# Second block's latent, pool and convolution projections from three products of split operands, quarter by quarter

## The reference, cut to what matters

```python
h = rmsnorm_2(x, norm1_g[l]) * (1.0 + sc1) + sh1          # (256, 1024)
proj = h @ w_in[l]                                         # (1024, 5792)
cq, ckv, kr, pu, cx, cb, cc, gl = jnp.split(proj, IN_OFFSETS, axis=-1)
ya = mla_branch(cq, ckv, kr, ...)      # latent attention, 384 + 256 + 32 columns
yb = pool_branch(pu, ...)              # 512 columns
yc = conv_branch(cx, cb, cc, ...)      # 3 x 512 columns
gates = sigmoid(gl + b_gate)           # 3 x 1024 columns
```

## Time and profile before

| | us |
|---|---|
| median of 3 runs | 2551.68 |
| lowest, highest | 2546.58, 2554.73 |
| the profiled execution's own time | 2548.41 |
| span of its instructions | 2546.4 |
| TensorE matmuls busy | 2051.8 |
| VectorE busy | 864.3 |
| ScalarE busy | 594.8 |

### The profile page before, as it was taken

One profiled execution on the slowest core, in us unless ns is written; L12 is line 12 of the kernel. 1 busy time (PEld: TensorE's weight loads), 2 busy tenths in 40 slices (PEclk: granted clock), 3 DMA queues, 4 the chain that ended last, 5 costly groups with the idle time before them and its releaser, 6 DMA issues.

```text
span 2546.4 us, 34316 instructions
## 1 busy us (share of the span) xinstructions
PE 2051.8 (81%) x14184; PEld 1362.8 (54%) x14184; DVE 864.3 (34%) x1599; ACT 594.8 (23%) x1001; POOL 32.0 (1%) x50
## 2 busy tenths in 40 slices
PE   7877889998998997999876666665999976666765
PEld 6756657877756885788542222222778652222221
DVE  4645564665554664244220000002144230010002
ACT  3222234441123442064210010001054120000000
POOL 0010000000000000000000000000000000000000
PEclk9989899998998998999888887887999988888787
DMA  8201034766963665432459999999332439999996
GB/s 309 102 1 35 2 109 155 265 242 208 329 240 137 251 250 176 149 133 100 165 223 427 426 427 425 426 427 387 134 132 93 201 153 426 427 426 427 426 426 283
DMA packets 150299, 641.76 MB, mean 252 GB/s; under 512 B 9310, under 2 KB 30840, under 8 KB 117046
## 3 DMA queue, kind: packets, MB, share of 16 engines
q1 hardware_dynamic: 143898, 637.13, 63.0%
q10 hardware_dynamic: 6300, 3.20, 0.5%
HBM read 639.21 MB, written 1.10 MB: 251 GB/s over the span
## 4 chain that ended last, share of the span: by engine, by line
PE 55%; DMA 31%; DVE 6%; ACT 3%; issue 2%; DVEq 1%; POOL 1%; SPq 0%; ACTq 0%; POOLq 0%
DMA ring<-in_w_down 31%; PE psum L1189 5%; PE psum L844 5%; PE psum L846 5%; PE psum L845 5%; PE psum L1304 4%; PE psum L1100 3%; PE psum L1089 3%; PE psum L942 3%; PE psum L616 2%; PE psum L1179 2%; PE psum L823 2%; PE psum L647 1%; PE psum L959 1%; PE psum L737 1%
## 5 line engine op out<-in xcount | busy, mean ns | idle before, releaser
L1284 PE MATMUL psum<-ring,arena 128*32 128x256 f32 x4096 | 298.0, 442 | 185.1 <-DMA ring<-in_w_up 146.1
L1284 PEld LDWEIGHTS psum<-ring,arena 128*32 128x32 f32 x4096 | 143.5, 123 | 341.5 <-issue 155.6
L1304 PE MATMUL psum<-ring,arena 128*32 128x512 f32 x1024 | 166.9, 784 | 94.1 <-DMA ring<-in_w_down 84.8
L844 PE MATMUL psum<-arena_r 128*128 128x512 f32 x512 | 207.8, 406 | 13.9 <-DVE arena_r L1650 7.1
L846 PE MATMUL psum<-ring_r,arena_r 128*128 128x512 f32 x512 | 205.0, 400 | 0.0
L1991 DVE TENSOR_TENSOR arena<-psum,arena 128x256 f32<-128x256 f32 x32 | 13.6, 425 | 559.0 <-PE psum L1284 559.0
L1384 DVE TENSOR_TENSOR ring_r<-ring,arena_r 128x2048 fp32r<-128x2048 f32 x64 | 143.8, 2288 | 87.0 <-ACT arena_r L2049 87.0
L2392 ACT ACT_TABLE_LOAD x32 | 41.1, 1283 | 514.3 <-PE psum L1284 514.3
L1998 DVE COPY arena<-psum 128x512 f32<-128x512 f32 x64 | 44.3, 692 | 273.0 <-PE psum L1304 271.8
L2049 ACT CAST arena_r<-ring 128x2048 fp32r<-128x2048 f32 x64 | 119.6, 1904 | 71.8 <-PE psum L846 71.8
L1304 PEld LDWEIGHTS psum<-ring,arena 128*32 128x32 f32 x1024 | 32.8, 126 | 191.4 <-DMA ring<-in_w_down 101.5
(11 more groups left out here) (379 smaller groups left out, 3026.1 us busy)
## 6 DMA issues: line engine op xcount, KB each, us to landing
ring<-in_w_gate SPq DMA_DIRECT2D x64, 2048.0 KB, 26.6
ring<-in_w_up SPq DMA_DIRECT2D x64, 2048.0 KB, 26.1
ring<-in_w_down SPq DMA_DIRECT2D x64, 2048.0 KB, 26.3
ring<-in_mlp_w SPq DMA_DIRECT2D x32, 2048.0 KB, 8.7
ring<-in_w_mod SPq DMA_DIRECT2D x24, 2048.0 KB, 11.2
ring<-in_w_in SPq DMA_DIRECT2D x20, 2048.0 KB, 8.1
ring<-in_gdn_w_in SPq DMA_DIRECT2D x8, 2048.0 KB, 17.9
ring<-in_dswa_w_in SPq DMA_DIRECT2D x9, 1536.0 KB, 14.4
```

Of the source, the lines that this page charges most:

```text
L844: mm(o, xh, wh, start=start, stop=False, skip_group_check=True)
L1284: ins = mm(PS[32 * j:32 * j + 32, 4 + m, 0:T], XGE[:, 4 * u + kk, :], W(v + 2 * m + u, D)[:, kk, j * T:(j + 1) * T], start=u == 0 and kk = ...
L1304: ins = mm(PS[32 * j:32 * j + 32, (7, 4)[half], :], HTE[:, k % 2, 32 * (k // 2):32 * (k // 2) + 32], W(v + 4 + u, D)[:, j, half * 512:(hal ...
```

## The change

All projections of that group but the first (`V_CQ`, which stays float32) are computed as three fp32r products, as the gates are. The weights are split quarter by quarter: 5 ring units with 4 quarters each make 20 quarters per layer, numbered q = 0 to 19. For the two units that `tok` computed (`V_KV`, `V_PU`) a quarter is two of the eight 128-row chunks over all columns; for the other three a quarter is 128 columns over all rows. ScalarE casts a quarter into one of three buffers (`WP`, in parts of the arena that hold other things later), VectorE writes the rest in place into the slot, TensorE waits for the count of `w_lo` and multiplies. A buffer is reused when TensorE has signalled the quarter three before (`half_used`, or the slot's release at a unit's last quarter). VectorE also makes the low part of the activations, `HL_R`, in an area of its own ahead of everything else; the later subtraction into `HT_R` (L1866) stays. The counts of `hi` and `w_lo` that the gates wait for are raised by 20 per layer. Nothing is changed in SyncE's and GpSimd's streams.

```diff
+        hl_at = q_at + 4 * T + 4 * 258
+        P1_UNITS = ((V_KV, C_PU - QR), (V_PU, 512), (V_CX, 512), (V_CC, 512), (V_CB, 512))
+        NQ = 4 * len(P1_UNITS)
+        WP = [gr_at, mixt_at, ot_at]
+        HL_R = ar_r[:, hl_at:hl_at + KC * T].rearrange("p (k n) -> p k n", k=KC)
...
+        def part_high(q):
+            w, wide = WP[q % 3], P1_UNITS[q // 4][1]
+            if q < 8:
+                return ar_r[:, w:w + 2 * wide].rearrange("p (k c) -> p k c", k=2)
+            return ar_r[:, w:w + KC * P].rearrange("p (k c) -> p k c", k=KC)
+        def part_of(slot, q):
+            wide, j = P1_UNITS[q // 4][1], q % 4
+            v = slot[:, 0:KC * wide].rearrange("p (k c) -> p k c", k=KC)
+            return v[:, 2 * j:2 * j + 2, :] if q < 8 else v[:, :, j * P:(j + 1) * P]
...
         @block.tensor
...
+                def three(o, a, b, start, stop):
+                    (ah, al), (bh, bl) = a, b
+                    mm(o, ah, bh, start=start, stop=False, skip_group_check=True)
+                    mm(o, al, bh, start=False, stop=False, skip_group_check=True)
+                    return mm(o, ah, bl, start=False, stop=stop, skip_group_check=True)
+                def part_done(ins, q):
+                    if q % 4 == 3:
+                        used(ins, u2 + P1_UNITS[q // 4][0])
+                    else:
+                        ins.then_inc(sem("half_used"), 1)
+                def tok_split(i, b):
+                    w = P1_UNITS[i][1]
+                    for q in range(4 * i, 4 * i + 4):
+                        pe.wait_ge(sem("w_lo"), L * (NQ + 24) + q + 1 + 64)
+                        wh, wl = part_high(q), part_low(q)
+                        for t in range(TT):
+                            ts = slice(t * P, (t + 1) * P)
+                            for kk in range(2):
+                                k = 2 * (q % 4) + kk
+                                ins = three(bank(b + t, w), (XH_R[:, k, ts], HL_R[:, k, ts]), (wh[:, kk, :], wl[:, kk, :]),
+                                            k == 0, k == KC - 1)
+                            if q % 4 == 3 and t == 0:
+                                ins.then_inc(sem("tok_mm"), 1)
+                        part_done(ins, q)
-                def feat(n, b):
-                    full(pe, u2 + n, tu)
-                    for ch in range(4):
+                def feat(i, b):
+                    for q in range(4 * i, 4 * i + 4):
+                        pe.wait_ge(sem("w_lo"), L * (NQ + 24) + q + 1 + 64)
+                        wh, wl = part_high(q), part_low(q)
+                        o = pair(b + (q % 4) // 2, T)[:, q % 2]
                         for k in range(KC):
-                            ins = mm(pair(b + ch // 2, T)[:, ch % 2], W(u2 + n, 512)[:, k, ch * P:(ch + 1) * P], HT[:, k, :],
-                                     start=k == 0, stop=k == KC - 1, skip_group_check=True)
-                    used(ins, u2 + n)
+                            ins = three(o, (wh[:, k, :], wl[:, k, :]), (XH_R[:, k, :], HL_R[:, k, :]), k == 0, k == KC - 1)
+                        part_done(ins, q)
                 tok(V_CQ, QR, 0)
-                tok(V_KV, C_PU - QR, 2)
-                tok(V_PU, 512, 4)
-                feat(V_CX, 6)
+                tok_split(0, 2)
+                tok_split(1, 4)
+                feat(2, 6)
                 pe.wait_ge(sem("ckv_out"), L + 1)
                 pe.wait_ge(sem("sq2"), L + 1)
-                feat(V_CC, 0)
-                feat(V_CB, 2)
+                feat(3, 0)
+                feat(4, 2)
...
         @block.vector
...
+                dve.wait_ge(sem("x_hi"), L + 1)
+                v.tensor_tensor(HL_R, HT[:], XH_R.bitcast(F32), ALU.subtract)
+                def part_rest(q):
+                    dve.wait_ge(sem("hi"), L * (NQ + 24) + q + 1 + 64)
+                    v.tensor_tensor(part_low(q), part_weight(q), part_high(q).bitcast(F32), ALU.subtract).then_inc(sem("w_lo"), 1)
+                for q in range(3):
+                    part_rest(q)
                 for t in range(TT):
...
                     v.tensor_copy(CQ[:, t, 0:QR], bank(t, QR)).then_inc(sem("cq_out"), 1)
+                for q in range(3, 6):
+                    part_rest(q)
...
                 ins.then_inc(sem("ckv_out"), 1)
+                part_rest(6)
+                part_rest(7)
                 dve.wait_ge(sem("sq2"), L + 1)
...
+                part_rest(8)
                 dve.wait_ge(sem("rs2"), L + 1)
...
                 ins.then_inc(sem("cqn_ready"), 1)
+                part_rest(9)
+                part_rest(10)
...
                     v.tensor_copy(MK[:, t, :, NOPE:DQK], bm(KR[:, t, :], MH))
+                for q in range(11, 18):
+                    part_rest(q)
                 dve.wait_ge(sem("cx_out"), L + 1)
                 spent(dve, u2 + V_CC, tu)
...
                 settle()
+                part_rest(18)
                 for ch in range(4):
                     v.tensor_scalar(BCT[:, ch, :], CZ[:, ch, 0:T], CW[:, ch:ch + 1], None, ALU.mult)
+                part_rest(19)
...
                 ins.then_inc(sem("conv_y"), 1)
-                dve.wait_ge(sem("x_hi"), L + 1)
                 v.tensor_tensor(HT_R[:], HT[:], XH_R.bitcast(F32), ALU.subtract).then_inc(sem("x_lo"), 1)
...
         @block.scalar
...
+                def part_high_of(q):
+                    if q % 4 == 0:
+                        full(act, u2 + P1_UNITS[q // 4][0], tu)
+                    if q >= 3:
+                        p = q - 3
+                        if p % 4 == 3:
+                            spent(act, u2 + P1_UNITS[p // 4][0], tu)
+                        else:
+                            act.wait_ge(sem("half_used"), L * 3 * len(P1_UNITS) + 3 * (p // 4) + p % 4 + 1 + 32)
+                    a.copy(part_high(q), part_weight(q)).then_inc(sem("hi"), 1)
+                for q in range(3):
+                    part_high_of(q)
                 for i, (b, w) in enumerate(((0, QR), (2, KVR))):
+                    if i == 1:
+                        for q in range(3, 7):
+                            part_high_of(q)
...
                 a.copy(ajunk[:], SS2[:, 3:4]).then_inc(sem("sq2"), 1)
+                for q in range(7, 11):
+                    part_high_of(q)
...
                 ins.then_inc(sem("pu_out"), 1)
+                for q in range(11, 15):
+                    part_high_of(q)
...
                 ins.then_inc(sem("cx_out"), 1)
+                for q in range(15, NQ):
+                    part_high_of(q)
```

More of the change, by code:

```diff
@@ L321, in program @@
         PU = c(TT, 512)
+        mixt_at = c.at
         MIXT = c(4, T)
         BCT = c(4, T)
+        ot_at = c.at
         OT = c(4, T)
@@ L328, in program @@
         KT = c(MH, T)
+        hl_at = q_at + 4 * T + 4 * 258
+        assert hl_at + KC * T <= 20480
+        P1_UNITS = ((V_KV, C_PU - QR), (V_PU, 512), (V_CX, 512), (V_CC, 512), (V_CB, 512))
+        NQ = 4 * len(P1_UNITS)
+        WP = [gr_at, mixt_at, ot_at]
+        HL_R = ar_r[:, hl_at:hl_at + KC * T].rearrange("p (k n) -> p k n", k=KC)
         c = Carve(sec_top)
@@ L535, in W, with part_weight, part_low @@
             return ring[n % RING][0:parts, 0:a * b].rearrange("p (a b) -> p a b", b=b)
+        def part_high(q):
[7 more added lines that the diff above has]
+            return v[:, 2 * j:2 * j + 2, :] if q < 8 else v[:, :, j * P:(j + 1) * P]
+        def part_weight(q):
+            return part_of(ring[(U_SEC + P1_UNITS[q // 4][0]) % RING], q)
+        def part_low(q):
+            return part_of(ring_r[(U_SEC + P1_UNITS[q // 4][0]) % RING], q)
         def gate_weight(s):
@@ L1182, in gate @@
                             used(ins, wu)
-                    pe.wait_ge(sem("w_lo"), L * 24 + s + 1 + 64)
+                    pe.wait_ge(sem("w_lo"), L * (NQ + 24) + NQ + s + 1 + 64)
                     if s == 0:
@@ L1864, in _ @@
                 ins.then_inc(sem("conv_y"), 1)
-                dve.wait_ge(sem("x_hi"), L + 1)
                 v.tensor_tensor(HT_R[:], HT[:], XH_R.bitcast(F32), ALU.subtract).then_inc(sem("x_lo"), 1)
                 def gate_rest(s):
-                    dve.wait_ge(sem("hi"), L * 24 + s + 1 + 64)
+                    dve.wait_ge(sem("hi"), L * (NQ + 24) + NQ + s + 1 + 64)
                     v.tensor_tensor(gate_low(s), gate_weight(s), WQ[s % 3].bitcast(F32), ALU.subtract).then_inc(sem("w_lo"), 1)
```

## The result

| | median us | runs (lowest to highest) |
|---|---|---|
| before | 2551.98 | 4 (2546.58 to 2554.73) |
| changed | 2519.39 | 4 (2518.50 to 2525.24) |

The ratio is 0.9878, 95% interval 0.9862 to 0.9894: 32.6 us faster between the medians, with 27 to 35 us in the interval. The forecast was 2528 with a range of 2521 to 2540. The profiled execution took 2518.50 us (span 2516.5), 29.9 less than the one before.

A forecast was written before the change was run, and what follows sets the result against it. TensorE alone was taken to bound the projections: 62.94 us removed, 51.6 added, 11.35 gained per layer, 22.7 for two. That gave 2525.7 from the profile, 2529.0 from the median; forecast 2528, range 2521 to 2540.

The forecast's parts named there:

- TensorE alone bounds the stretch, and the stretch gains the difference of its instructions: Projections: TensorE sets the end, the other engines have room; gain 11.35 us per layer, 22.7 us for two.
- The sum of the changed part: TensorE work added per layer in the projections: 34.08, 11.15 and 6.36 us, sum 51.6 us, replacing 62.94 us.
- The 288 columns: Key/value products: 48 of 288 columns at 132.6 ns, on a line between two measured widths, 6.36 us per layer.
- the subtractions of 576 elements: VectorE's rests of the key/value quarters: between 0.685 and 1.217 us each, taken as 0.75.
- The splits are hidden, q4 is the tightest point: Casts and rests run beside TensorE's projections without making it wait; least room at the pool input's first quarter, 0.5 us.
- The experts' stage moves ahead unchanged: Expert stage in both layers: starts earlier with the projections, because its load stream waits for TensorE; length unchanged.
- Behind the projections all is as before: Stages after the projections: nothing changes, convolution sums are done before `V_CB` ends, L1866 keeps its 2.28 us.
- TensorE streams fp32r as closely as float32: Rival, projections: products take half a float32 instruction, 47.2 us per layer, gain 31.4, so 2517 to 2520; chance 0.03.
- The hand-over rival: Projections: each of 20 quarters pays 0.28 us waiting for its rest, 11.2 us in all, 2539; chance 0.09.
- the chain as a bound: Rival, projections: TensorE waits a full split round each time, 35 us more per layer than gained, about 2619; chance 0.04.
- the gain is lost later: Rival: loads of the next stages come into each other's way, time within 7 us of before; chance 0.05.

The follow-up runs named there:

- pad4: The changed kernel with the last quarter's products repeated four more times per layer, putting the TensorE time back; 2549.70 us, ratio 0.9995 to the kernel before.
- cast3b: The changed kernel with each of ScalarE's casts made three times over, with a drain between them; 2544.80 us, ratio 0.9971 to the kernel before.

## Why the prediction was right and where it failed

- *TensorE alone bounds the stretch, and the stretch gains the difference of its instructions.* Right: 22.7 us between the profiles, and pad4, which takes that time back, leaves nothing of the gain.
- *The sum of the changed part.* Right to a tenth of a microsecond: 51.6 against 51.66. The 288 columns, which no row showed, came out on the line between 256 and 512. For the subtractions of 576 elements the prediction worked out 0.76 us beside the 0.75 that it took; they measured 0.755. Its formula gives ns and not cycles, and a row did bear on it: 1024 elements make 1.224 us by it, and the earlier trace rows has 1.217.
- *The splits are hidden, q4 is the tightest point.* Right: no wait with three buffers, 2.3 us with two (2.2 expected), 10.3 with threefold casts (10.4).
- *The experts' stage moves ahead unchanged.* Right: 460.5 to 460.7 us in both profiles.
- *The turn of the layer loop* was taken as unchanged. It is 0.7 us longer, 9.6 to 9.7 us in the profiles of all kernels with the change and some 9.0 in those without. The prediction had no term for it, nor for the second norm, which is as much shorter over the two layers; neither cause was tried.
- *"Behind the projections all is as before": this step failed.* It priced at 0 what measured, between the first two profiles, 5.5 us ahead of the experts and 2.6 between the projections and the second norm. Those stages are not of fixed length. They contain TensorE work that begins at 1.2 GHz behind idle time (0.50 granted), and how much of it runs so differs between kernels and between executions of one kernel. The Trainium skill ("TensorE: Matmul & The Clock Gate", What's actually happening) has the low clock as the default that activity releases, which the rows agree with (0.50 behind a stretch without TensorE work, 1.00 later); it also says that the moment isn't tied to the kernel's start, by which the lengths should be drawn anew in each run. The 37.1 and 38.1 us of the changed kernel's two profiles fit that. But three executions with the timing of the kernel before (two of it, one of pad4) gave 41.2, 41.4 and 41.3 us in layer one and 38.4 in layer two each time, which chance alone makes unlikely; three are too few to exclude it, and cast3b, whose projections end only 0.8 us sooner, had 38.6 in layer one. So the part of the saving above 22.7 us was not foreseen by any term. The prediction looked at the granted clock in the stretches that change and had the earlier trace rows 0.79 from 1280 to 1300 us, ahead of the experts, in hand; it read only the DMA share from that row and did not ask which unchanged stages run partly cold.
- *The rival "TensorE streams fp32r as closely as float32"* gave 2517 to 2520 and so hit the measured time by a mechanism that is not there: the fp32r spacing stayed at 118 to 119 ns. The hand-over rival (2539) and the chain as a bound are refuted by the absence of waits; cast3b shows what the latter looks like. That the gain is lost later is refuted by the time and the experts' unchanged length.

The cause of the surplus is shown as far as this: between the first two profiles it lies in unchanged stages whose products run slower at the lower granted clock; it goes to 0 when TensorE's work is put back; and filling the idle time ahead of the experts in both kernels leaves a gain of 27.1 us with the long filling and 20.5 with the short one, each some 6 us either way, where it was 32.6 and 28.1 without. That the whole surplus is the clock's is therefore likely and not shown. In the second pair of profiles the gain is 21.0 us, so the surplus is not in every execution. What sets the moment at which the clock rises, and why the kernel before meets the long case in layer one in two profiles of two, stays open.

## What to carry to other kernels

Where one engine fills a stretch without a gap, count its instructions by the rows of its nearest shapes; a line between two sizes was good here for a third. Then list the unchanged stages whose TensorE work starts behind idle time at 1.2 GHz, and widen the range on the side of gain and loss by what their products would take at the other clock: here some 4 us per layer. If such stages exist, a few products that nobody reads, at the right place, may be a cheap gain: nine per layer gave the kernel before 11.2 us, a third of what this change gave. They gave the changed kernel nothing that can be told, and too many of them gave nothing to either.

## What the runs showed of the hardware that was not expected

- The spacing of fp32r products is longer than half a float32 instruction of the same width at the same granted clock of 1.00: 118.3 to 118.7 ns at 256 columns, 132.7 at 288, 231 at 512, against 107.9, 121 and 215. Three of them still cost some 18 to 19% less than the two float32 instructions that they replace.
- The granted clock stayed at 0.50 through the router, 32 instructions of 16 columns in 7.02 us, though TensorE is marked busy for 3.77 of 4 us there. With nine filling products per layer, most of them ahead of it, the router took 5.0 to 5.8 us in three stages of four and 7.03 in the fourth.
- The stretch ahead of the experts took few lengths: over nine profiles without filling, 18 stretches, it was 37.0 to 37.1, 38.1 to 38.6 or 41.0 to 41.4 us, and nothing between.
